# MLP down projections by seven block products for eight, with the weights' block sums formed on the chip

## The reference, cut to what matters

```
def sqrelu_mlp(h, w_up, w_down):
    return jnp.square(jax.nn.relu(h @ w_up)) @ w_down
...
xp = xp + sqrelu_mlp(rms_norm(xp, mlp_norm_g[i]), mlp_w_up[i], mlp_w_down[i])
xs = xs + sqrelu_mlp(rms_norm(xs, mlp_norm_g[i]), mlp_w_up[i], mlp_w_down[i])
```

## Time and profile before

| | us |
|---|---|
| median of 3 runs (1586.68 to 1588.81) | 1587.51 |
| profiled execution | 1590.08 |
| its span | 1588.3 |
| PE busy | 1542.5 (97%) |
| POOL busy | 764.7 (48%) |
| DVE busy | 613.1 (39%) |
| ACT busy | 382.3 (24%) |

### The profile page before, as it was taken

The page is one execution under the profiler, slowest core; times in us unless marked ns, Lnnn a source line. Parts: engine busy times, 40 slices in busy tenths (PEclk is TensorE's granted clock), DMA queues, the critical chain, the costliest instruction groups (busy, mean ns, idle before and its releaser), DMA issues.

```text
span 1588.3 us, 29034 instructions
## 1 busy us (share of the span) xinstructions
PE 1542.5 (97%) x10920; PEld 1460.2 (92%) x10920; DVE 613.1 (39%) x874; ACT 382.3 (24%) x875; POOL 764.7 (48%) x481
## 2 busy tenths in 40 slices
PE   6999999999999999999989999999999999999999
PEld 4778999999999999999976878787999999999998
DVE  6004726754314123134545455554454132141231
ACT  3323201122102011022237465665122011020110
POOL 6355454454555555555645052341355555555552
PEclk9999999999999999999999999998999999999999
DMA  7222232222222222222332010101122222222221
GB/s 233 67 69 77 66 116 79 66 80 80 81 80 80 82 90 80 79 79 83 125 94 71 1 54 1 53 13 40 42 78 81 88 84 80 79 80 87 84 78 48
DMA packets 36369, 120.16 MB, mean 76 GB/s; under 512 B 6040, under 2 KB 6744, under 8 KB 36064
## 3 DMA queue, kind: packets, MB, share of 16 engines
q1 hardware_dynamic: 30528, 110.25, 22.1%
q10 hardware_dynamic: 5792, 9.23, 1.9%
HBM read 115.91 MB, written 3.55 MB: 75 GB/s over the span
## 4 chain that ended last, share of the span: by engine, by line
PE 94%; DVE 2%; ACT 2%; issue 1%; DMA 0%; ACTq 0%; DVEq 0%
PE ps L539 28%; PE ps L541 27%; PE ps L540 27%; PE ps L868 2%; PE ps L847 2%; PE ps L803 1%; PE ps L637 1%; PE ps L876 1%; DVE neg_max L1222 1%; ACT kT L1487 1%; PE ps L806 1%; PE ps L817 1%; PE ps L788 1%; PE ps L744 1%; PE ps L706 0%
## 5 line engine op out<-in xcount | busy, mean ns | idle before, releaser
L484 POOL TENSOR_SCALAR w_hi<-raw 128x1024 fp32r<-128x1024 f32 x208 | 221.2, 1063 | 618.2 <-PE ps L541 615.2
L486 POOL TENSOR_TENSOR w_lo<-raw,w_hi 128x1024 fp32r<-128x1024 f32 x208 | 505.3, 2429 | 17.3
L539 PE MATMUL ps<-hid_hi,w_hi 128*128 128x288 f32 x1408 | 417.7, 297 | 2.1 <-DVE hid_lo L1146 2.1
L540 PE MATMUL ps<-hid_lo,w_hi 128*128 128x288 f32 x1408 | 416.0, 295 | 0.0
L541 PE MATMUL ps<-hid_hi,w_lo 128*128 128x288 f32 x1408 | 414.7, 295 | 0.0
L539 PE MATMUL ps<-h_hi,w_hi 128*128 128x288 f32 x1280 | 380.6, 297 | 0.0
L540 PE MATMUL ps<-h_lo,w_hi 128*128 128x288 f32 x1280 | 377.6, 295 | 0.0
L541 PE MATMUL ps<-h_hi,w_lo 128*128 128x288 f32 x1280 | 376.3, 294 | 0.0
L539 PEld LDWEIGHTS ps<-hid_hi,w_hi 128*128 128x128 f32 x1408 | 264.5, 188 | 2.3 <-issue 2.2
L541 PEld LDWEIGHTS ps<-hid_hi,w_lo 128*128 128x128 f32 x1408 | 265.8, 189 | 0.0
L540 PEld LDWEIGHTS ps<-hid_lo,w_hi 128*128 128x128 f32 x1408 | 265.0, 188 | 0.0
(11 more groups left out here) (155 smaller groups left out, 1664.3 us busy)
## 6 DMA issues: line engine op xcount, KB each, us to landing
raw<-stream SPq DMA_DIRECT2D x208, 512.0 KB, 3.5
out_x<-x ACTq DMA_DIRECT2D x8, 288.0 KB, 2.2
x<-xt ACTq DMA_DIRECT2D x4, 288.0 KB, 7.3
x<-xt SPq DMA_DIRECT2D x4, 288.0 KB, 8.2
b_bc<-bs ACTq DMA_DIRECT2D x2, 512.0 KB, 6.6
cache_raw<-cache_ct ACTq DMA_DIRECT2D x1, 1024.0 KB, 4.9
v_out<-sgu_grow ACTq DMA_DIRECT2D x1, 512.0 KB, 4.5
ws_sb<-ws ACTq DMA_DIRECT2D x2, 256.0 KB, 4.6
```

Of the source, the lines that this page charges most:

```text
L484: nc.gpsimd.tensor_scalar(w_hi[:, u, :], raw[:, u, :], 1.0, 0.0, ALU.mult, ALU.add).then_inc(split_hi, 1)
L486: nc.gpsimd.tensor_tensor(w_lo[:, u, :], raw[:, u, :], w_hi[:, u, :].bitcast(F32), ALU.subtract).then_inc(split_lo, 1)
L539: nc.tensor.matmul(out, l_hi, r_hi, start=first, stop=False)
L540: nc.tensor.matmul(out, l_hi, r_lo, start=False, stop=False)
```

## The change

The down projection of a quarter is a product of a 1024 x 1024 block of weights with 1024 hidden features by 576 tokens. It is now cut into 2 x 2 blocks on every side (512 output features by 512 hidden features, and 288 tokens), and the eight block products are replaced by seven, in Winograd's form, which needs sums of blocks of both operands. The work goes by pairs: pair i makes the output tiles i and i+4 (units 8+2i and 9+2i of the quarter), with seven `product` calls of 4 slices x 3 matmuls of 128 x 288.

What it asks of each engine:

- PE: products 0, 1, 2 open banks Z, X, Y; product 3 adds to Z, 4 to X, 5 opens Y again, 6 adds to X. Before 3, 4, 5 and 6 it waits for DVE's reading of the bank (`tile_read`). A product also waits for the low part of its weight block.
- DVE: sums of the hidden operand in `up` (three subtractions of 288 columns for two tiles, and one more for the first), low parts of the seven operands, four sums of weight blocks per pair (`add_weights`), two of seven low weight blocks (`low_block`), and seven additions to `x` per pair. The weight sums of pairs 0 and 1 are formed in the up tiles 4, 6 and 7; those of pair i+2 between the additions of pair i. A weight sum waits for both raw units of its pair.
- ACT: the casts of weights in the MLPs (formerly POOL's), of units in the up part and of blocks in the down part, and the casts of the seven operands.
- POOL: in the MLPs only low parts, five of the seven blocks of a pair and the up units.
- SP: the units of the down pairs 2 and 3 and the first four of the next quarter are loaded when all low blocks of the pair two before are made, by POOL and by DVE.

The host orders the units of an MLP as 0, 4, 1, 5, 2, 6, 3, 7, so that a block's two tiles are neighbours. All other stages keep their work, with semaphore counts shifted; the input projection of the latent attention takes its slices in the order j, j+4.

```diff
+            def product(i, p, op, bank, opens, ready):
+                for k in range(PAIRS):
+                    if k == PAIRS - 1:
+                        pe.wait_ge(hid_ready, ready)
+                    w = slice((p % 2) * 512 + k * P, (p % 2) * 512 + k * P + P)
+                    out, first, last = ps[:, bank, 0:TH], opens and k == 0, k == PAIRS - 1
...
+                            product(par, 2, 2, Y, True, hid + 2)
+                            pe.wait_ge(split_lo, low + 2)
+                            pe.wait_ge(tile_read, t0)
+                            product(par, 3, 3, Z, False, hid + 2)
+                            pe.wait_ge(low_set, dve_low + 1)
+                            pe.wait_ge(tile_read, t0 + 1)
+                            product(par, 4, 4, X, False, hid + 3)
...
+                def add_weights(q, i, n):
...
+                    if n == 0:
+                        for slot in (top, low):
+                            dve.wait_ge(raw_loaded[slot], q * 64 + loads_of(unit0 + 8 + 2 * i))
+                        nc.vector.tensor_tensor(s1, a21, a22, ALU.add).then_inc(w_sum_set, 1)
...
+                        add(0, i + 4, second, Z)
+                        sum_ahead(0)
+                        add(1, i, first, X)
...
+                        sum_ahead(1)
+                        add(2, i, first, Y)
+                        if i + 1 < PAIRS:
+                            low_block(q, i + 1, DVE_LOW[0])
+                        add(3, i, second, Z)
+                        sum_ahead(2)
+                        add(4, i, second, X)
+                        sum_ahead(3)
+                        add(5, i + 4, first, Y)
...
+                for j in range(12, 16 if last else 20):
+                    i = (j - 12) // 2
+                    sp.wait_ge(split_lo, q * Q_LOW + (low0 + 4 + (i + 1) * len(POOL_LOW)))
+                    sp.wait_ge(low_set, q * Q_DVE_LOW + (dve_low0 + (i + 1) * len(DVE_LOW)))
+                    sp.dma_start(raw[:, j % SLOTS, :], stream[q * 16 + (unit0 + j)]).then_inc(raw_loaded[j % SLOTS], 16)
```

More of the change, by code:

```diff
@@ L194, in build_trunk @@
         krr = place("krr", [P, NT, QK], F32, b_at + 4 * (NT + 1) * LAT)
+        v_at = region(4 * NT * DS)
         raw = new("raw", [P, SLOTS, UNIT])
@@ L380, in bank_of, with block_of, factor, loads_of @@
             return t - 3 if t >= 3 else 2 + 3 * (chunk % 2) + t
+        def block_of(w, b):
+            return w[:, b // 2, (b % 2) * 512:(b % 2) * 512 + 512]
+        def factor(i, b):
+            top, low = 2 * i % SLOTS, 2 * i % SLOTS + 1
+            sums = w_sum[:, i % 2]
+            return (sums[:, 0, :], raw[:, top, 0:512], raw[:, top, 512:UNIT], sums[:, 2, :], sums[:, 1, :],
+                    raw[:, low, 512:UNIT], raw[:, low, 0:512])[b]
+        def loads_of(unit):
+            return unit // SLOTS * 16 + 16
         def key_rows(j):
@@ L579, in norm_spread, with token_chunk @@
                 last.then_inc(rms_spread, 1)
-            def token_chunk(chunk, parity, first_unit, width, between=None, h_count=None, tiles=None):
+            def token_chunk(chunk, parity, first_unit, width, between=None, h_count=None, tiles=None, halves_apart=False):
                 for j in range(4):
@@ L644, in _ @@
                         feature_tile(u, f, f + U_SGU, HID, hid_ready, half * 8 + (B_SGU + 8))
[L647 to L654, removed]
-                        norm_sums(s)
[L657 to L661, removed]
+            def product(i, p, op, bank, opens, ready):
[4 more added lines that the diff above has]
+                    out, first, last = ps[:, bank, 0:TH], opens and k == 0, k == PAIRS - 1
+                    l_hi, l_lo = w_hi[:, p // 2, w], w_lo[:, p // 2, w]
+                    r_hi, r_lo = op_hi[:, op, k, :], op_lo[:, op, k, :]
+                    nc.tensor.matmul(out, l_hi, r_hi, start=first, stop=False, skip_group_check=True)
+                    nc.tensor.matmul(out, l_hi, r_lo, start=False, stop=False, skip_group_check=True)
+                    done = nc.tensor.matmul(out, l_lo, r_hi, start=False, stop=last, skip_group_check=True)
+                done.then_inc(unit_done, 1)
@@ L1384, in _ @@
+                with act.Fori(0, 3, 1) as q:
+                    up(q)
+                    down(q, None, True)
+                up(3)
+                down(3, last_s, last_s is not None)
+            mlp(F_MLP0, D_MLP0, U_MLP0, 0, 0, 0, B_MLP0, 0, 1, 1, 2)
             act.dma_start(cache_raw[:], cache_ct).then_inc(cache_loaded, 16)
@@ L1560, in _units, with _feature_major @@
     return out
-def _feature_major(w, rows, n_tiles):
-    return _units(*[(w[rows:rows + 8 * P, m * P:(m + 1) * P], 8, P) for m in range(n_tiles)])
+def _feature_major(w, rows, tiles):
+    return _units(*[(w[rows:rows + 8 * P, m * P:(m + 1) * P], 8, P) for m in tiles])
 def _weight_stream(sgu_in, sgu_out, up, down, mla_in, uq, ukv, wo):
@@ L1573, in _weight_stream @@
     for half in range(2):
-        units += _feature_major(sgu_in[:, half * D:(half + 1) * D], 0, 8)
-        units += _feature_major(sgu_out, half * D, 8)
+        units += _feature_major(sgu_in[:, half * D:(half + 1) * D], 0, range(8))
+        units += _feature_major(sgu_out, half * D, range(8))
     def mlp(layer):
@@ L1593, in _weight_stream @@
         units += _units((both, 2, 512))
-    units += _feature_major(wo, 0, 8)
+    units += _feature_major(wo, 0, range(8))
     units += mlp(1)
```

350 lines of the change are left out of this document (278 added, 72 removed).

## The result

The changed kernel takes 1628.9 us in the median of 4 runs (1624.5 to 1635.2), the kernel before 1588.2; the ratio is 1.0251, with a 95% interval of 1.0229 to 1.0273. It is slower by 40.7 us, inside the range of 1600 to 1682; the forecast was 1647.5. The profiled execution took 1632.6 us (span 1630.8).

The account below looks back on a forecast made before the run. PE's matmul queue was taken to bound the kernel. Per quarter -6.40 + 9.06 (load chains) + 4.0 (POOL) + 0.7 (clock) = +7.36 us, times 8 plus 1 about +60: 1650, less 2.6 for the median, 1647.5 us; range 1600 to 1682.

Parts of the forecast that it names:

- PE's saving: In each quarter's down part, 336 matmuls instead of 384 at 0.133 us each: 6.40 us less, if PE never waits.
- The load chain into pair 0: From up tile 7 through casts, low block, loads, sum and addition to product 4: 12.97 us, due at 6.40, wait 6.57.
- The load chain into pair 1: From product 6 of pair 0 through low block and loads to pair 1's wait: 8.89 us, due at 6.40, wait 2.49.
- DVE against POOL: DVE's two-input SBUF instructions held by POOL's subtractions between up tile 4's eviction and the first addition: 4.0 us per quarter.
- the 7.5 worked out without POOL: Pair 0's first addition, which product 3 awaits, comes at about 7.5 us, due at 4.8: wait 2.7, contained in 6.57.
- The clock: PE's granted clock falls to half around the waits: 0 to 1.7 us lost per quarter, taken as 0.7.
- The rest: In the first MLP's last quarter, eight next-stage operands stand among the waits: 1 us; other parts nothing shown.
- The rival of the load chains alone: DVE and POOL miss each other and the clock stays: +2.66 us per quarter, 1609 us; chance 17%.

Follow-up runs that it names:

- the fast version without POOL's blocks: Changed kernel with weight sums two pairs ahead and pair 1's last two sums moved later, and POOL's low blocks cut to 32 of 512 columns: 1541.4 us.
- e2: Changed kernel with only pair 1's last two weight sums moved, from behind up tile 7 to behind pair 0's first addition: 1636.1 us, ratio to before 1.0289.
- e4: Changed kernel with unread matmuls filling PE's waits, 32 ahead of pair 0's product 3, 12 ahead of product 4 of pairs 0 and 1: 1616.8 us.
- e1: Changed kernel with the weight sums two pairs ahead moved behind the fifth addition of a pair and later: 1609.8 us, ratio to before 1.0108.
- e5: Changed kernel with POOL's five low blocks of a pair cut to 32 of 512 columns: 1595.3 us, ratio to before 1.0039.
- the version with both moves: Changed kernel with sums two pairs ahead moved to later additions and pair 1's last two sums behind pair 0's first and second additions: 1573.0 us.
- the last experiment: Seven-product version with DVE's additions first, next pair's last two weight sums one addition later, first low block behind the fourth: 1561.4 us, ratio to before 0.9814.

## Why the prediction was right, by its own steps

**PE's saving, 6.40 us per quarter:** right. The distances stayed at 0.133, the up part at 51.20, and the fast version without POOL's blocks has a quarter of 96.8.

**The load chain into pair 0, 12.97 us:** measured 12.99. That it fits to 0.02 us is luck, since links came out 1.25 us longer and others 1.23 us shorter. DVE's eviction began 1.03 us after the up part instead of 0.20 (POOL had held a weight sum before it), and POOL's low block took 1.62 instead of 1.20; on the other side the path from the eviction to the last cast took 3.64 instead of 4.08, the two loads were usable 4.90 us after the low block instead of 5.41 with the hand-overs, and the cast, the sum, the addition and the last hand-over took 0.3 less. The e2 and e4 runs show that this chain, and not the amount of work ahead of the first addition, sets product 4; the e1 run shows that the other chain ends only 0.32 us before it.

**The load chain into pair 1, 8.89 us:** measured 8.39. Over all eight quarters the lateness at product 4 of the two pairs is 9.05 us, where 9.06 was forecast; single quarters lie between 8.4 and 10.1.

**DVE against POOL, 4.0 us per quarter:** mis-sized. The mechanism is there (e5: means back to 0.69 to 0.72 us). But on the chain to product 4 it added only the 1.25 us of the two links named above, and those are already in the 12.99. The larger part, 2.1 us on the two sums ahead of the first addition, made product 3 late (9.62 against the 7.5 worked out without POOL), and product 3's lateness is contained in that of product 4. I had added 4.0 on top of the two chains, as if every late instruction of DVE's lengthened one of them. Without POOL's low blocks the kernel is 34 us faster, 4.2 per quarter, but that contains POOL's own 1.2 us in each chain, which the forecast had in its 9.06.

**The clock, 0.7 us:** mis-sized; 1.7 by the run with the filled waits, the upper end of the 0 to 1.7 that were given. I had taken it that PE mostly still waits in such a stretch. In the quarter shown the two low stretches last 6.8 and 3.4 us, the first begins inside the wait and reaches over product 4, and the second falls on product 5 of pair 1, which had nothing to wait for.

**Waits behind product 4:** the sum had no term for them. With the clock full they are 1.0 us per quarter (e4); in the changed kernel the low clock covers most of them, and the two together are 2.70.

**The rest, 1 us:** too small. The down part of the fourth quarter took 59.4 us against 55.3 to 56.1 in the first three, 3.4 to 4.1 us above them.

Together: forecast 9.06 + 4.0 + 0.7 = 13.76 of excess per quarter, measured in the second quarter 8.58 (POOL's 1.25 in it) + 1.7 of clock + 1.0 of later waits = 11.28. Eight times the difference is 20 us, and the forecast was 18.6 too high. The rival of the load chains alone, 1609, is 20 too low, since it left out the clock and the later waits. The measured time lies halfway between the two, so it does not choose between them by itself: the direction and the load chains were right by their mechanism, while POOL's term was too large and what stands for the clock and the later waits too small, and these errors partly cancel.

By the Trainium skill's "SBUF — State Buffer", section "SBUF: two separate sides", the lock is exclusive and held for the whole instruction. An instruction of DVE's would then be either free or delayed by what is left of a subtraction. The trace agrees: of the 192 weight sums and low blocks of DVE in the changed kernel 127 took about 0.69 us and the others 1.3 to 1.8, none between.

## What to carry to other kernels

When work is taken from the engine that sets the time, look at what feeds it at the seams: here 6.4 us less of matmuls per quarter met a chain of cast, low part, load, sum and addition that was 6.6 us late. An instruction that waits for a load must not stand in a queue ahead of the small one that frees a PSUM bank; the same instructions in another order were worth 67 us (1628.9 to 1561.8). Where two chains end at one place, removing the shorter one gains nothing, and a delay must be added to the longer one only. When engines wait for each other, price the low clock by a run in which the waits are filled, since short waits hide beneath it.

## What the runs showed of the hardware

DVE and POOL, when both have two-input work in SBUF without a break, take turns: DVE's 512-column instruction goes from 0.69 to 1.4 us and POOL's from 1.28 to about 1.7, and in the rows of the last experiment DVE's sum at 517.64 and the next one at 519.35 each end 0.55 us after a subtraction of POOL's (518.51 and 520.21). DVE's additions, which read PSUM, stayed at 0.45 us. An idle stretch of PE of 1.07 us in the version with both moves left the clock at 1.00 for the whole quarter, and one of 1.63 us in its fourth quarter was followed by a clock of 0.50; in the changed kernel one of 4.42 us and one of 1.83 were each followed by matmuls at half clock (0.50), for 6.8 and 3.4 us, the second time beginning 1.6 us after the wait had ended. A filler of useless matmuls kept it at 1.00 and gave back 1.7 us per quarter. PE's first matmul behind the 4.42 us wait lasts 0.61 us, behind the 1.83 us wait 0.40.
